# Constant products on TensorE in three of its waits, in a three-layer f32 kernel on one core

## The reference

```
for i in range(2):                                   # first block
    proj = x @ w_in[i]                               # q, k, v, latents, gates
    o_na, o_mla = neighborhood_attention(...), latent_attention(...)
    merged = sigmoid(g_na + b) * (o_na @ w_na_o) + sigmoid(g_mla + b) * (o_mla @ w_mla_o)
    x = layer_norm(ALPHA * x + merged @ w_out[i])
    f = swiglu(x) if i == 0 else moe_swiglu(x)       # 8 experts, top 2, of width 3584
    ple = sigmoid(x @ w_ple_gate[i]) * (p[i] @ w_ple[i])
    x = layer_norm(ALPHA * x + f + ple)
# second block: rms norm, four kinds of attention or convolution, w_out, rms norm, swiglu
```

## Time and profile before

| | |
|---|---|
| time, median of 3 executions | 2018.38 us (2018.35 to 2020.46) |
| the profiled execution, span from the first to the last instruction | 2018.5 us |
| TensorE busy with products | 1982.4 us, 98% of the span, 10728 records |
| VectorE / ScalarE / GpSimd busy | 1603.9 / 1017.1 / 59.0 us |
| mean granted TensorE clock | 0.996 |
| DMA | 553.15 MB, mean 274 GB/s |

### The profile page before, as it was taken

The page is one execution under the profiler, slowest core; times in us unless marked ns, Lnnn a source line. Parts: engine busy times, 40 slices in busy tenths (PEclk is TensorE's granted clock), DMA queues, the critical chain, the costliest instruction groups (busy, mean ns, idle before and its releaser), DMA issues.

```text
span 2018.5 us, 27225 instructions
## 1 busy us (share of the span) xinstructions
PE 1982.4 (98%) x10728; PEld 1676.7 (83%) x10728; DVE 1603.9 (79%) x1618; ACT 1017.1 (50%) x1047; POOL 59.0 (3%) x53
## 2 busy tenths in 40 slices
PE   8999999999999999999999999999999998999999
PEld 7988788889988778888888888888888887868887
DVE  3676688886666698888888888888888975668987
ACT  0264110021453377777777777777777753472000
POOL 0110100000000200000000000000000000100000
PEclk9999999999999899999999999999999999999999
DMA  9643588753634589999999999999999985445650
GB/s 322 195 164 110 181 296 315 271 165 122 211 124 178 222 298 384 380 380 370 384 384 377 384 380 379 373 385 384 382 384 371 408 287 164 135 126 167 205 175 37
DMA packets 184217, 553.15 MB, mean 274 GB/s; under 512 B 9296, under 2 KB 112080, under 8 KB 140864
## 3 DMA queue, kind: packets, MB, share of 16 engines
q1 hardware_dynamic: 175296, 517.55, 69.7%
q10 hardware_dynamic: 6912, 25.02, 3.2%
q0 software_dynamic: 1920, 9.34, 1.2%
HBM read 528.02 MB, written 23.59 MB: 273 GB/s over the span
## 4 chain that ended last, share of the span: by engine, by line
PE 93%; DVE 3%; ACT 3%; issue 1%; DMA 0%; DVEq 0%; ACTq 0%; SPq 0%
PE act_ps L1190 30%; PE dve_ps L1215 15%; PE act_ps L1040 9%; PE job_ps L1144 6%; PE act_ps L1112 4%; PE dve_ps L1112 4%; PE dve_ps L916 4%; PE dve_ps L1040 2%; PE act_ps L1087 2%; PE job_ps L1067 2%; PE act_ps L1111 2%; PE dve_ps L1111 2%; PE act_ps L916 1%; PE job_ps L1198 1%; PE job_ps L967 1%
## 5 line engine op out<-in xcount | busy, mean ns | idle before, releaser
L2482 DVE TENSOR_TENSOR weights_rest<-weight_ring,expert_short 128x2048 fp32r<-128x2048 f32 x336 | 762.9, 2289 | 103.2 <-ACT expert_short L1781 102.6
L1781 ACT ACTIVATE expert_short<-weight_ring 128x2048 fp32r<-128x2048 f32 x336 | 641.0, 1916 | 109.9 <-PE act_ps L1190 74.1
L1190 PE MATMUL act_ps<-expert_short,tokens_short 128*128 128x512 f32 x896 | 354.2, 395 | 3.9 <-ACT arena_o L1798 2.0
L1190 PE MATMUL act_ps<-expert_short,tokens_rest 128*128 128x512 f32 x896 | 349.2, 390 | 0.0
L1190 PE MATMUL act_ps<-weights_rest,tokens_short 128*128 128x512 f32 x896 | 349.1, 390 | 0.0
L1190 PEld LDWEIGHTS act_ps<-expert_short,tokens_short 128*128 128x128 f32 x896 | 168.2, 188 | 38.7 <-DVE weights_rest L2482 3.2
L1190 PEld LDWEIGHTS act_ps<-expert_short,tokens_rest 128*128 128x128 f32 x896 | 168.2, 188 | 36.3
L1190 PEld LDWEIGHTS act_ps<-weights_rest,tokens_short 128*128 128x128 f32 x896 | 168.4, 188 | 33.6
L1767 ACT ACTIVATE arena_mla<-arena_mla 128x512 f32<-128x512 f32 x22 | 14.0, 634 | 298.4 <-DVE arena_mla L2415 298.4
L2402 DVE TENSOR_TENSOR weights_rest<-weight_ring,ffn_weights_short 128x2048 fp32r<-128x2048 f32 x66 | 151.3, 2292 | 2.2
L1215 PE MATMUL dve_ps<-expert_short,hidden_short 128*128 128x512 f32 x440 | 137.1, 393 | 0.0
(11 more groups left out here) (421 smaller groups left out, 3518.3 us busy)
## 6 DMA issues: line engine op xcount, KB each, us to landing
weight_ring<-in_moe_w SPq DMA_DIRECT2D x336, 1024.0 KB, 6.8
weight_ring<-in_w_in SPq DMA_DIRECT2D x43, 1024.0 KB, 8.0
weight_ring<-in_ffn_w SPq DMA_DIRECT2D x32, 1024.0 KB, 7.8
weight_ring<-in_w_out SPq DMA_DIRECT2D x12, 1024.0 KB, 6.8
weight_ring<-in_w_gate SPq DMA_DIRECT2D x11, 1024.0 KB, 5.3
weight_ring<-in_w_up SPq DMA_DIRECT2D x11, 1024.0 KB, 8.1
weight_ring<-in_w_down SPq DMA_DIRECT2D x10, 1024.0 KB, 7.0
weight_ring<-in_w_ple_gate SPq DMA_DIRECT2D x8, 1024.0 KB, 6.2
```

Of the source, the lines that this page charges most:

```text
L1190: m = nc.tensor.matmul(bank[0:CAP, :], a[:, 4 * c + k, :], w[:, k, :], start=(c == k == i == 0), stop=(c == 1 and k == 3 and i == 2))
L1781: nc.scalar.activation(shorts[u % SHORTS][:, :], ring[:, slot, half], ACT.Copy).then_inc(moe_w_short, 1)
L2482: V.tensor_tensor(ring_lo[slot][:, half], ring[:, slot, half], shorts[u % SHORTS][:, :], ALU.subtract)\
```

## The change

GpSimd clears the first eighth of `work` at once. TensorE makes six f32 products of these zeros with 256 columns at its begin; five products of the identity with constants, also of 256 columns, behind the first layer's last down product; and eight of them behind `put_back(1)` of the last expert. They write to a PSUM bank that nobody reads until its next product starts afresh. One semaphore is new, and one wait in front of each of the first two places.

```diff
+START_BUSY, NORM_BUSY, LAST_BUSY = 6, 5, 8
...
-        last_columns = sem("last_columns")
+        last_columns, busy_cleared = sem("last_columns"), sem("busy_cleared")
...
# GpSimd, its first instruction
+            nc.gpsimd.memset(work[:, 0, :], 0.0).then_inc(busy_cleared, 1)
             pool.wait_ge(consts_loaded, 32)
...
# TensorE, the end of experts(turn)
                 put_back(1)
+                keep_busy(act_ps[0], LAST_BUSY)


             pe.wait_ge(x_here[0], 16)
...
                 if k == DT // 2:
                     pe.wait_ge(weights_here[0], 32)
                 return x_here[k // (DT // 2)], 16
+            def keep_busy(bank, count):
+
+                for _ in range(count):
+                    nc.tensor.matmul(bank[:, 0:SEQ], const("ident"), consts[:, 0:SEQ], start=True, stop=True)
+            pe.wait_ge(busy_cleared, 1)
+            for _ in range(START_BUSY):
+                nc.tensor.matmul(act_ps[0][:, 0:SEQ], work[:, 0, 0:P], work[:, 0, :], start=True, stop=True)
             for l in range(LAYERS):
...
                     swiglu(FT, None)
+                    pe.wait_ge(dve_tile_done, n.d - 1)
+                    keep_busy(dve_ps[n.d % 2], NORM_BUSY)
                     pe.wait_ge(act_tile_done, n.a)
                     turn_rows(2 * l + 1, act_ps + job_ps[0:2])
```

## The result

| | before | after |
|---|---|---|
| time, median of 8 executions each | 2018.37 us (2016.37 to 2020.46) | 2023.92 us (2021.61 to 2024.81) |
| ratio | | 1.0026, 95% interval 1.0017 to 1.0035 |
| profiled execution: its own time | 2020.46 us | 2024.81 us |
| profiled execution: its span | 2018.49 us | 2023.0 us |
| TensorE busy with products | 1982.4 us, 10728 records | 1987.9 us, 10766 records |

The changed kernel is slower by 5.5 us of the medians, 3.4 to 7.1 by the interval of the ratio. The spans of the two profiled executions differ by 4.5 us. One thing said ahead of the prediction was wrong: an execution's own time isn't its span. Of all executions of this case that have both, it is 1.8 to 2.3 us more, and 3.1 in one. So the profiled execution of before, with its own time of 2020.46, was one of the longer ones of its kernel, 2.1 us over the median.

The account below looks back on a forecast made before the run. TensorE was taken to bound the kernel (93% of the last-ending chain). 2018.5 + 2.6 (begin) - 1.2 (norm) - 0.7 (behind the experts) = 2019.2, forecast as 2019.1 us by the median; range 2016.4 to 2023.4.

Parts of the forecast that it names:

- the side to which I gave 0.14: Whole kernel: chance given to a measurement slower by more than 0.2% (4.0 us); same had 0.83, faster 0.03.
- The begin, +2.6: Kernel start: 12 new records run behind the weights' wait and must be made up at full pace, +2.6 us.
- zeros wake the engine: Begin: the rival denied this, with full clock 5.1 us later and 2021.7 us in all; chance 0.06.
- The case in which the begin does what the change says: Begin: products run ahead of the weights' arrival, cost nothing and gain up to 3.3 us; 2013.2 to 2016.5, chance 0.06.
- The norm, -1.2: Behind the first layer's last down product: filled wait prevents half clock, -1.2 us, bounds -0.45 and -1.7.
- The router's stretch: Half clock from 677.9 to 688.2 us: a third, worth 1.7 us, may go or come; taken as 0.
- Behind the experts, -0.7: Behind the last put_back: new products cost nothing and hold the clock for the transposes, -0.7 us, bounds 0 and -1.2.
- turned rows again at 1674.2, cost 0: Behind the experts: the branch begins later, but its instruction packet leaves at the same moment, so turned rows aren't delayed.
- the drain of the queue: Behind the experts, rival: the branch waits for all queued products, +3.45 us, 2023.2 by the median; chance 0.15.
- the upper bound of 1.3: Behind the experts: most the products could cost, the branch's full delay of 1.3 us passed on to the turned rows.
- The clock's gain, -0.7: Behind the experts: with 0.9 us of stand left, no half clock at the turned rows, -0.7 us.
- The clock falls all the same: Norm and behind the experts, rival: idle ends or transposes still drop the clock, neither gain comes, 2021.0; chance 0.12.

Follow-up runs that it names:

- e2: The changed kernel with 40 more instructions in the jumped-over body of If(more > 0), shifting the branch's target; 2018.67 us, ratio 1.0000 to the kernel before.
- e8: The kernel before with the jumped-over body of If(more > 0) cut to one product, so the branch's target is near; 2016.32 us, ratio 0.9988.
- e6: The kernel before plus only the begin's six products of zeros, placed ahead of the waits for x and the first weights; 2017.58 us, ratio 0.9994.
- e4: The kernel before plus only the five products behind the first layer's last down product; 2018.02 us, ratio 0.9995.
- e5: The kernel before plus only the eight products behind the experts, in the turn that is run; 2018.51 us, ratio 1.000.
- e10: The kernel before with 40 more instructions in the body of If(more > 0) that is not run; 2018.62 us, ratio 1.000.
- e9: The kernel before plus six begin products ahead of the waits, five at the norm, six behind the experts in the run turn only; 2015.27 us, ratio 0.9987.
- e7: The kernel before plus six begin products ahead of the waits and five at the norm, none behind the experts; 2016.40 us, ratio 0.9987.
- e1: The kernel before with 108 more instructions in the body of If(more > 0) that is not run; 2023.22 us, ratio 1.0023.
- e3: The kernel before plus only the begin's six products of zeros, behind the two waits; 2022.37 us, ratio 1.0016.

## Why the prediction was wrong

Forecast 2019.1 (2016.4 to 2023.4), measured 2023.92: outside the range and on the side to which I gave 0.14. In the pair of traces the three places came to +2.6 - 1.2 + 4.4, where the forecast had +2.6 - 1.2 - 0.7, and the stretch between the norm and the experts gave -1.4.

**The begin, +2.6: right**, to the record: start at 6.26, copy at 15.58. Its premise, full clock at the same moment, isn't fixed: the two traces happened to agree on it, and so does the pair e2 and e8, but the moment moves by 2.3 us between executions. That zeros wake the engine as data does is shown by the same sum, and that rival falls: without it the copy would have come past 17. The case in which the begin does what the change says falls too; e6 shows that even in the right place it is worth 0.8 to 1.7 us and not up to 3.3, as the second half of the weights is then late. I had only taken its 0.40 us of idle as a bound at the old pace.

**The norm, -1.2: right in the trace** (-1.23, no half clock), too much for the median. My sum started from one execution that had the fall; five of the seven traces without the products have it, e6 and e8 have not. The same holds for the comparison with the median: I set the sum against the span of 2018.5 and took off 0.1, when that execution's own time was 2020.46. The difference of +0.7 was put on the right median by that, but as if the profile were the usual execution. That the profile was 2.1 us over the median was the sign that it had lost more to the clock than the usual execution. The router's stretch, taken as 0 with ±1.7, gave -1.4 in the pair of traces; it is 3.4, 6.8 or 10.2 us long in the traces of this case, and the third stretch of the table goes with it: 1209.3 us with 10.2 (before, e4, e5, e6, e8, e10), 1207.8 or 1207.9 with 6.8 (after, e9), 1206.5 or 1206.7 with 3.4 (e2, e7). I take it as spread of executions; that the change has no part in it wasn't tested. The medians' +5.5 against the traces' +4.5 fits an ordinary execution of before that has less of both to gain, which was not tested further.

**Behind the experts, -0.7: this is the step that failed**, at "turned rows again at 1674.2, cost 0" and in what it left out. Measured +4.4.

- The late branch. It began 0.98 us late (I had 1.3), with the drain of the queue not waited for, so that rival falls by its mechanism: by it the branch could have begun only at 1673. Its time, 2023.2, was the nearest to the result, and for another reason. But the fetch didn't leave at the same moment: the packet moved with the branch, from 3.4 to 4.65 us behind `put_back`, and in e5 the turned rows came 1.31 later with nothing else changed. So the upper bound of 1.3 was about the value (+1.15 in the changed kernel, 1.31 in e5), and in e2, where the branch itself took 0.7 longer, it was passed (1.70). I had read the packet's place behind SyncE's load as cause. e8 shows what the length of the branch hangs on: with a near target it is 0.22 us.
- The end of the fetched code, which no term priced: 3.1 us of stand and then 3.4 us of half clock. My sum had taken it that behind the branch the turned rows run as before. e1 shows the stand without any product, e2 takes it away without taking a product, e10 shows that 40 instructions more in the jumped code aren't it. The Trainium skill ("Runtime: NRT & Kernel Launch", Instruction fetch mechanics) states that code comes in blocks of 16 KiB, 256 instructions, and that the next block is fetched while the current one is executed. I used its sentence on the taken branch and not this one. The packets of 0.02 MB agree with it. But the next block isn't at hand in time behind a branch that lands some 30 instructions ahead of a block's end: there the 15 pairs last 1.9 us and the stand is 3.1.
- The clock's gain, -0.7 with bounds 0 and -1.2, was the right size: e5 has 0.9 (1.31 late in, 0.37 late out), e9 has 1.0 with nearly no delay. In the changed kernel it was spent: the stand let the clock fall behind the products that were to hold it.

**The clock falls all the same**: not at the norm, and not at the turned rows of e5 and e9 (0.11 us from start to start). The Trainium skill's rule that transposes don't count as busy ("TensorE: Matmul & The Clock Gate", Part 4: PE-mode transpose) was one thing that spoke for this rival; the granted clock stayed 1.00 through the sixteen transposes of e9, so for the 1.7 us that they last here it isn't borne out. It did fall behind the stand of 3.1 us, where TensorE did nothing.

**What stays open.** e3's median is 1.5 us over the 2.6 that its place costs. What sets the moment of full clock at the begin between 10.0 and 12.4 us, the length of the router's stretch and whether the norm loses the clock, wasn't found; together they are worth up to some 5 us (1.1, 2.8 and 1.2), enough for the 4 us by which the executions of the kernel before spread. Nor was it found what holds the first packet for 3.3 us and more, and what sets the second one's moment, 9.1 to 9.8 us behind `put_back` however late the branch is.

## What to carry to other kernels

A taken branch over much code has two prices on TensorE: the fetch of its target (6 us here), which starts when the branch is reached and so is delayed by whatever fills the queue ahead of it, and, where the first piece of code ends too soon behind the target, a stand until the next piece is there (3.1 to 3.4 us here). Any edit ahead of the target, executed or not, moves that place; so read the trace for a stand released by "issue" behind every branch, and try a shift of the target before a product is blamed. An instruction packet alone proves nothing: the kernel before had both and no stand. Filler work belongs ahead of the wait that it is to bridge, no longer than that wait, and its gain ends where the next load is late; and a profile that lies over its kernel's median can show losses that the usual execution doesn't have.

## What the runs showed of the hardware

- The branch goes while products of before are still queued: with 4 and 16 pairs of weight load and product ahead it began 0.00 and 0.07 us behind `put_back`'s second half, with 20 pairs 0.98.
- The same branch took 5.8 to 6.8 us with a far target in eleven traces, and 0.22 us with a near one.
- Code that is never executed made this kernel 4.9 us slower (e1), and it took 3.7 us off the place behind the experts in the changed kernel (e2).
- Products of zeros bring TensorE from 1.2 to 2.4 GHz like products of data: with them started at 1.10 us, real products ran at the full pace from 6.30.
